# Gathering the token rows of two 64-expert mixtures on TensorE instead of through DRAM

## What is computed

```python
def hier_moe(h, w_rg, b_rg, w_re, b_re, w_gate, w_up, w_down, ws_gate, ws_up, ws_down, w_sg):
    xt = h.reshape(-1, D)                                   # 512 tokens x 1024
    g_sel = jnp.argmax(xt @ w_rg + b_rg, axis=-1)           # one of 8 groups
    ...                                                     # top 2 of the 8 experts of that group, softmax gates
    buf = jnp.zeros((P, D), xt.dtype).at[dest].set(xt[tok_sorted])     # rows of each expert together
    ...
    hid = jax.nn.silu(xb @ w_gate[e]) * (xb @ w_up[e])      # per expert: 1024 -> 256
    return hid @ w_down[e]                                  # 256 -> 1024
    ...
    y = jnp.zeros((N, D), xt.dtype).at[tok_sorted].add(out[dest] * gate_sorted[:, None])
    ys = (jax.nn.silu(xt @ ws_gate) * (xt @ ws_up)) @ ws_down          # shared expert, 1024 -> 512 -> 1024
    y = y + jax.nn.sigmoid(xt @ w_sg) * ys
```

## Time and profile before

| | |
|---|---|
| three runs | 2607.84, 2610.89, 2621.81 us (median 2610.89) |
| span of the profiled execution | 2608.0 us |
| share of the span: PE, DVE, ACT, POOL | 83%, 48%, 30%, 8% |
| DMA over the span | 684.69 MB, mean 263 GB/s |
| first 64-expert mixture | about 1036 to 1562 us |
| second 64-expert mixture | about 2039 to 2604 us |

### The profile page before, as it was taken

One profiled execution on the slowest core, in us unless ns is written; L12 is line 12 of the kernel. 1 busy time (PEld: TensorE's weight loads), 2 busy tenths in 40 slices (PEclk: granted clock), 3 DMA queues, 4 the chain that ended last, 5 costly groups with the idle time before them and its releaser, 6 DMA issues. The chain is left out here.

```text
span 2608.0 us, 43437 instructions
## 1 busy us (share of the span) xinstructions
PE 2153.1 (83%) x18242; PEld 1504.7 (58%) x18242; DVE 1246.3 (48%) x1974; ACT 776.7 (30%) x1304; POOL 210.0 (8%) x204
## 2 busy tenths in 40 slices
PE   5999999896884999887778766899998887768766
PEld 3977777794542789443334335677777644334433
DVE  3367676645223544543333336666545653233334
ACT  4266666432113323211111114444423411111112
POOL 2010000101001000000000002111111000000001
PEclk8999999998997999998889888999999999889988
DMA  9157675439997323899999973211113699999995
GB/s 356 46 195 245 219 245 188 130 98 365 420 421 266 97 97 126 352 411 416 419 419 417 415 320 98 58 46 46 50 50 130 258 386 416 415 414 420 409 417 205
DMA packets 211851, 684.69 MB, mean 263 GB/s; under 512 B 23022, under 2 KB 122039, under 8 KB 152503
## 3 DMA queue, kind: packets, MB, share of 16 engines
q1 hardware_dynamic: 198742, 646.01, 64.3%
q0 software_dynamic: 8912, 21.04, 2.2%
q10 hardware_dynamic: 3984, 14.68, 1.4%
HBM read 671.68 MB, written 21.00 MB: 266 GB/s over the span
## 5 line engine op out<-in xcount | busy, mean ns | idle before, releaser
L221 PE MATMUL PS<-second 128*128 128x256 f32 (+1 forms) x4944 | 929.8, 346 | 54.5 <-DVE second L251 21.7
L221 PEld LDWEIGHTS PS<-second 128*128 128x128 f32 x4944 | 760.1, 193 | 200.8 <-DVE second L251 29.1
L221 PE MATMUL PS<-ring,arena 128*32 128x256 f32 (+5 forms) x6288 | 670.2, 457 | 208.4 <-DMA ring<-in_moe_w_down 65.6
L221 PEld LDWEIGHTS PS<-ring,arena 128*32 128x32 f32 (+2 forms) x6288 | 317.1, 125 | 445.8 <-issue 306.2
L221 PE MATMUL PS<-arena 128*32 128x256 f32 (+10 forms) x2480 | 500.6, 386 | 76.7 <-DMA ring<-in_moe_w_up 20.3
L221 PEld LDWEIGHTS PS<-arena 128*32 128x32 f32 (+4 forms) x2480 | 248.4, 153 | 243.4 <-issue 173.5
L233 ACT ACTIVATE arena<-PS 128x256 f32<-128x256 f32 (+2 forms) x218 | 106.6, 489 | 575.3 <-PE PS L221 497.9
L240 DVE TENSOR_TENSOR arena<-PS,arena 128x512 f32<-128x512 f32 (+1 forms) x305 | 210.6, 690 | 98.5 <-PE PS L221 71.4
L240 DVE TENSOR_TENSOR arena<-arena,PS 128x256 f32<-128x256 f32 (+1 forms) x77 | 41.0, 532 | 403.6 <-PE PS L221 402.4
L233 ACT ACTIVATE arena<-arena 128x128 f32<-128x128 f32 (+4 forms) x299 | 176.3, 590 | 191.9 <-DVE arena L240 64.7
L240 DVE TENSOR_TENSOR second<-ring,second 128x1024 fp32r<-128x1024 f32 (+1 forms) x90 | 149.1, 1656 | 155.0 <-ACT second L233 149.1
(11 more groups left out here) (170 smaller groups left out, 1355.9 us busy)
## 6 DMA issues: line engine op xcount, KB each, us to landing
ring<-in_moe_w_down SPq DMA_DIRECT2D x124, 1024.0 KB, 14.3
ring<-in_moe_w_up SPq DMA_DIRECT2D x121, 1024.0 KB, 14.2
ring<-in_moe_w_gate SPq DMA_DIRECT2D x109, 1024.0 KB, 16.3
ring<-in_ada_w SPq DMA_DIRECT2D x48, 1024.0 KB
arena<-in_moe_w_gate SPq DMA_DIRECT2D x28, 1024.0 KB, 8.6
ring<-in_w_mod SPq DMA_DIRECT2D x22, 1024.0 KB, 9.8
arena<-in_moe_w_up SPq DMA_DIRECT2D x19, 1024.0 KB, 11.0
spare<-in_moe_w_gate SPq DMA_DIRECT2D x17, 1024.0 KB
```

What stands on the lines that cost most here:

```text
L221: return P.e.matmul(o, l, r, start=st, stop=sp)
```

## The change

The two 64-expert mixtures no longer store `XN` and no longer use indirect transfers. The 16-expert mixture keeps both. For each unit DVE builds a matrix `HOT` of 512 tokens by 128 rows (four blocks of 128 tokens): it compares the row numbers with each token's place, once for each of its two experts, multiplies by the token's 1/rms, and adds the two (`hot_ve`: nine instructions and one small one). `turn_pe` then makes the transposed rows directly, as products of the raw tokens `x` (stationary, every eighth feature of a row, so elements 32 bytes apart) with `HOT` (moving): 8 blocks of features by 4 blocks of tokens, 32 float32 products of 128 by 128 by 128 in place of eight transposes. DVE may start on its half after the first 16 of them.

In the head `turn_pe(0)` moves ahead of `tokens_pe` and of two steps of the shared expert. SP's wait for the store is gone. In `SIDE` the units 11 to 14 have 1, 1, 1, 1 steps in place of 2, 2, 0, 0. POOL's work in these mixtures is down to one row and the final products.

```diff
@@ new buffers
+    HOT = [view(16384 + 512 * i, 4, 128) for i in range(2)]
+    HOTB = spare[:, 2048:2560].rearrange("p (t r) -> p t r", t=4)
...
-    SIDE = (1, 2, 1, 2, 2, 1, 2, 1, 0, 2, 2, 2, 2)
+    SIDE = (1, 2, 1, 2, 2, 1, 2, 1, 0, 2, 2, 1, 1, 1, 1)
@@ begin_sp
-        S.wait_ge(at("xn_d", m.i), at("ps", "h2T", m.i, 3, 1))
+        S.wait_ge(at("ps", "h2T", m.i, 3, 1))
@@ turn_pe
+        if m.shared:
+            P.wait_ge(at("hot", m.i, n))
+            for k in range(8):
+                for t in range(4):
+                    i = mm((ba, bb)[k // 4][:, (k % 4) * 128:(k % 4) * 128 + 128], x[:, t, :].rearrange("q (p k) -> q k p", k=8)[:, k, :], HOT[n % 2][:, t, :], t == 0, t == 3)
+                if k % 4 == 3:
+                    i.then_inc(*P.mark("ps", "turn" if k == 7 else "turn0", m.i, n))
+            return
@@ moe_pe
         positions_pe(m)
         next(more, None)
+        if m.shared:
+            turn_pe(m, 0)
         tokens_pe(m, "tok", 0, m.NS)
...
@@ new: hot_ve, spots_ve
+    def hot_ve(m, n):
+
+        ts(m.near, m.spot, -128.0 * n, None, ALU.add, None)
+        V.wait_ge(at("ps", "turn", m.i, n - 2) if n > 1 else None, V.here())
+        for t in range(4):
+            for j, o in enumerate((HOT[n % 2], HOTB)):
+                V.e.tensor_scalar(o[:, t, :], iota[:, :], m.near[:, t, j:j + 1], rs[:, 4 + t:5 + t], ALU.is_equal, ALU.mult).then_inc(*V.mark())
+        tt(HOT[n % 2], HOT[n % 2], HOTB, ALU.add, "hot", m.i, n)
+
+    def spots_ve(m):
+        stt(m.spot, m.uu, 128.0, m.rr, ALU.mult, ALU.add)
@@ row_hots
         tt(m.rr, m.rr, m.ff, ALU.add)
+        if m.shared:
+            spots_ve(m)
+            if label[0] == "ohtok":
+                hot_ve(m, 0)
@@ moe_ve, in the loop over units, and in one(n) for the overflow units
+            if m.shared and n + 1 < m.NP:
+                hot_ve(m, n + 1)
             gate_up_ve(m, n)
...
         def one(n):
+            if m.shared:
+                hot_ve(m, n)
             turn_ve(m, n)
@@ h2T_ac
-        A.wait_ge(at("xn", m.before, t))
-        A.e.dma_start(xn_d[128 * t:128 * t + 128, :], XN[:, t, :]).then_inc(*D(f"xn_d{m.i}").next("xn_d", m.i))
+        if m.shared is None:
+            A.wait_ge(at("xn", m.before, t))
+            A.e.dma_start(xn_d[128 * t:128 * t + 128, :], XN[:, t, :]).then_inc(*D(f"xn_d{m.i}").next("xn_d", m.i))
```

More of the change, by code:

```diff
@@ L174, in program @@
     names_of_loads = ("xc", "xl", "stage", "rows", "z0", "z1", "zq", "x", "wba", "x2", "router0", "router1", "router2",
-                      "xn_d0", "xn_d1", "xn_d2", "y0", "y1", "xg0", "xg1", "xg2", "x_d", "out", "zero", "ab_d", "abp")
+                      "xn_d0", "y0", "y1", "xg0", "xg1", "xg2", "x_d", "out", "zero", "ab_d", "abp")
     d_sem = {n: sem("d_" + n) for n in names_of_loads}
     d_comb = [sem(f"d_comb{i}") for i in range(8)]
-    d_over = [[sem(f"d_over{j}_{i}") for i in range(n)] for j, n in enumerate((8, 8, 8))]
+    d_over = [[sem(f"d_over{i}") for i in range(8)]]
     def at(*label):
@@ L1448, in __init__ @@
                 self.tokf, self.ws = tmp(NB, 4), tmp(NB)
+                self.spot, self.near = tmp(4, 2), tmp(4, 2)
             self.tz, self.idx = tmp(NB), tmp(NB).bitcast(i32)
@@ L1824, in moe_pe @@
             row_pe(DIAG, ("row", m.i), state["side"])
-        turn_pe(m, 0)
+            turn_pe(m, 0)
         for n in range(m.NP):
@@ L1873, in turn_ve @@
         i, b = n % 2, bank("ta", m.i, n)
-        V.wait_ge(at("ps", "turn", m.i, n), at("ps", "gu", m.i, n - 2, 1) if n > 1 else None)
+        V.wait_ge(at("ps", "turn0" if m.shared else "turn", m.i, n), at("ps", "gu", m.i, n - 2, 1) if n > 1 else None)
         for k in range(4):
@@ L1982, in index_ve @@
         ts(m.tz[0:m.R, n0:n1], b, 0.0, 5000.0, ALU.is_equal, ALU.mult)
-        stt(m.idx[0:m.R, n0:n1], b, -1.0, m.tz[0:m.R, n0:n1], ALU.add, ALU.add, label, m.i)
         if m.shared:
             stt(m.tz[:, n0:n1], b, -1.0, m.tz[:, n0:n1], ALU.add, ALU.add, {"idx": "tokf", "idx2": "tokf2"}[label], m.i)
+        else:
+            stt(m.idx[0:m.R, n0:n1], b, -1.0, m.tz[0:m.R, n0:n1], ALU.add, ALU.add, label, m.i)
     def columns_ve(m, n0, n1):
@@ L2053, in route_ve @@
         ts(m.bb, m.pp, float(m.C), None, ALU.is_ge, None)
-        stt(m.rr, m.bb, 1000.0, m.pp, ALU.mult, ALU.add)
+        stt(m.rr, m.bb, 65536.0, m.pp, ALU.mult, ALU.add)
         row_hots(m, "ohtok", m.i)
-        index_ve(m, "tok", 0, m.NS, "idx")
+        if m.shared is None:
+            index_ve(m, "tok", 0, m.NS, "idx")
     def gates_of_ve(m, step):
@@ L2138, in moe_ve @@
         gates_of_ve(m, 0)
+        if m.shared:
+            turn_ve(m, 0)
+            index_ve(m, "tok", 0, m.NS, "idx")
         more_places_ve(m, 0)
         more = shared_ve(m) if m.shared else iter(())
-        turn_ve(m, 0)
+        if m.shared is None:
+            turn_ve(m, 0)
         gates_of_ve(m, 1)
@@ L2327, in moe_gp @@
         fill(m.M[:, 4:5], 0.0, "mz", m.i)
[L2328 to L2331, removed]
+        if m.shared:
+            G.wait_ge(at("sq2", m.before, 3), at("ps", "gu", m.i, 1, 1))
             row_gp(m.gate_col, DIAG, ("row", m.i))
[L2333 to L2343, removed]
             for t in range(4):
@@ L2347, in moe_gp @@
             return
+        for o in XG:
+            fill(o, 0.0, "zx", m.i)
+        G.wait_ge(at("sq2", m.before, 3))
+        row_gp(m.gate_col, DIAG, ("row", m.i))
+        for n in range(m.NP):
+            gather_gp(m, n)
+            if n == 6:
+                row_gp(colD[:, 64:72], DIAG, "frow", at("ps", ("row", m.i), 1))
+        count = count_of(m, G)
+        overflow(m, G, count, lambda n: gather_gp(m, n))
         G.wait_ge(at("yi", m.i), at("y", m.i, m.NB - 2), at("y", m.i, m.NB - 1))
@@ L2563, in gates_first_ve @@
     def gates_first_ve():
-        V.wait_ge(at("ps", "cm", 1, MO[1].NB - 1, 3, 1), at("passed", 1), V.here())
+        V.wait_ge(at("ps", "cm", 1, MO[1].NB - 1, 3, 1), V.here())
         V.e.memset(WBA[:, :, 16:32], 0.0).then_inc(*V.mark("wba0"))
```

## The result

The changed kernel takes 2843.8 us (median of 4 runs), the kernel before 2616.4 in the same session: a ratio of 1.088 (95% interval 1.0859 to 1.09), slower by some 228 us. The prediction was 2639 us, with a range of 2600 to 2700. The side was right; the size is that of rival B, and more than its outer end. The kernel before is timed anew in each session, and its median goes from 2611 to 2622 us between them, so sessions are best compared by their ratios.

A forecast was written before the change was run, and what follows sets the result against it. The weight stream was taken as the bound in the middle and end of mixtures, with PE slack there. First mixture +10.7, second +8.3 and overflow unit +8.7 us made 2639 us from 2610.9; range 2600 to 2700.

The forecast's parts named there:

- rival B: Turn's strided operand is slow: at 11.0 us a turn PE becomes the bound, 2673 us; chance 0.17.
- outer end: Strided operand at twice the price, 14.4 us a turn: 2787 us; chance 0.06, left out of the range.
- the term for the product: In each turn, 32 float32 products at 0.225 us take 7.2 us, 6.1 more per unit; no cost for the stride.
- My bound above, 1.5 times: Upper price of the strided read in the turn, from DVE's rows at this stride: 11.0 us a turn.
- Cover in the middle: Mid-mixture the turn costs nothing: a unit with two shared steps takes PE 29.8 us, the stream needs 30.2.
- 318 us: PE's work for all units of a mixture without turns, counted from the first gate product.
- The head: At each mixture's start, piece 3 of the shared weights is issued later: 8.8 us in the first, 9.0 in the second.
- Idle stream and gathers: Per mixture: stream idles for buffers in units 0 to 2, +11.2 and +8.6 us; removed gathers give -9.3 each.
- The overflow unit: At the end, one-hot, turn and combination delay gate 16 with no load covering it: +8.7 us.
- The sum: Whole kernel: 10.7 + 8.3 + 8.7 = +27.7 us on 2610.9, so 2639 us; chance 0.58.
- Rival C: Product is cheap, 0.13 us like a transpose, 4.2 us a turn: 2618 us, no change to tell; chance 0.12.
- D: Stream absorbs the head; PE's later turns don't reach it, only removed bytes count: 2592 us; chance 0.13.

The follow-up runs named there:

- contig: The changed kernel with the turn's stationary operand read as 128 features side by side, not every eighth (wrong features reach the experts): 2633.3 us, ratio 1.009 to before.
- stride2: The changed kernel with the turn's stationary operand read at every second element, 8 bytes apart (other features than the reference's): 2644.1 us, one time.
- stride4: The changed kernel with the turn's stationary operand read at every fourth element, 16 bytes apart (other features than the reference's): 2831.0 us, one time.
- no_gathers: The kernel before, without the indirect transfers of units 2 to 15 of both 64-expert mixtures (wrong expert inputs): 2591.5 us, ratio 0.9893.
- quarter: The contig kernel with only the first of four token blocks in each turn, 8 products in place of 32: 2594.9 us, one time.
- moving_contig: The changed kernel with the one-hot stationary and 512 side-by-side features moving, 8 products a turn (result not transposed, wrong data): 2630.8 us, one time.

## Why the prediction was right or wrong

- **The step that failed** is the term for the product: "Below, I take no cost", so 7.2 us a turn. It is 15.5. Of the two readings of DVE's rows that I wrote down, the one that I preferred (one element per cycle, so nothing to pay) doesn't carry over to PE. My bound above, 1.5 times, was taken from DVE too and was too low. The Trainium skill's rule stood on its page (Memory Cachelines) with no factor, and I gave it 0.17. Here contig, stride2 and stride4 show that two elements in 16 bytes or one is what decides, by a factor of 2.1.
- **Cover in the middle.** "In the middle of a mixture this costs nothing" hung on the 7.2. With 15.5 the 29.8 us of a unit become 38.1, and PE is the bound: rival B. Its arithmetic at 15.5 us a turn gives +97 us a mixture and +17 at the overflow unit, so some 2820. The measured +111.3, +103.7 and +17.6 show what it lacks: it prices work and no waits. The recorded terms of its 318 us add to 316. These plus 15 x 15.5 are 548.5 from the first gate product at 1091.0, so 1639.5, and the last weights are used at 1657.1. Between 1091 and 1657 PE waits 29.5 us in all, so the work itself was priced some 12 us too high. More than half of the waits, 16.3 us, are for DVE's copy of the hidden values; before, these were 3.6 us (from 1130 to 1560). The waits from 1130 to 1650 us:

```profile
PE PS L221 <- DVE arena L259: 16.3, 12, 2.3
PE PS L221 <- DMA ring<-in_moe_w_down: 5.7, 2, 4.5
```

- **The head.** In contig, where the turn has the price that I took, piece 3 comes 7.6 us later from the place product in the first mixture (forecast 8.8) and 11.8 in the second (forecast 9.0). Of this, 2.5 us are the clock, which the forecast had not: the same 98 records, from the turn on, took 15.11 us in the first at a granted clock of 1.00, and 17.63 in the second, where PE had waited 3.72 us before them and the clock was at 0.50 until 2074. Making `HOT` takes 3.1 us (forecast 2.9).
- **Idle stream and gathers.** From piece 3 to the last weights contig takes 0.7 us less than before in the first mixture (forecast +11.2 - 9.3 = +1.9) and 3.5 less in the second (forecast -0.7). With the 10.0 and 12.3 us that no_gathers saves there, the idle added is 9.3 and 8.8 us; the forecasts were 11.2 and 8.6.
- **The overflow unit** costs 11.2 us in contig, for 8.7: its turn took 9.36 us, not 7.2, since PE had waited 5.54 us and the clock was granted at 0.50 for the first 3.8 us of the turn. In the changed kernel it is 17.6.
- **The sum.** Forecast +28 us with a cheap turn: 2639. contig, which has it, took 2633, +21 us by both its median and its span. The terms measured above add to 26.4; the rest, -5.3, lies outside these stretches and has no cause that I can show. So the structure of the sum holds, and that the total came within 7 us is in part luck: -1.2 and +2.8 us in the two times of piece 3, -2.6 and -2.8 from there to the last weights, +2.5 at the overflow unit, and this -5.3.
- **A reading.** The earlier trace rows give 409 to 420 GB/s inside the two mixtures, not 410 to 422; nothing hangs on it.
- **Hidden work.** DVE's one-hots in the loop show no cost: the nine matrices that it makes between 1130 and 1500 us in the changed kernel are 32 us by their own durations, on an engine busy in 137 of 370, and PE waits for none of them there. Rival C falls (7.4 us a turn at best), and so does D: quarter shows all seven turns on the path.

## What to carry to other kernels

Before a product reads a float32 operand in place with a stride, ask how many of its elements share 16 bytes. With two the stationary operand cost 5% more, with one it cost twice, and at 32 bytes the moving operand cost twice too. A price seen on one engine is not that of another: 1.5 times on DVE, 2.1 on PE. Work moved to an engine with slack is free only as long as the unit stays under the stream's, so use it where the slack is: confined to the middle, the gather on PE made the kernel 0.8% faster; used in the heads and at the end too, where nothing covers it, 0.9% slower, even side by side. If a stretch is bound by loading, count its pieces as well as its bytes.

## What the runs showed of the hardware that I had not expected

- A float32 product of 128 by 128 by 128 takes 0.232 us with the stationary operand side by side, 0.244 at 8 bytes, 0.475 at 16 and 0.484 at 32.
- A moving operand of 512 elements pays the same: 0.446 us a record at 4 bytes, 0.933 at 32.
- The strided turn does not feel PE's clock. At the overflow unit PE has waited 5.54 us in both kernels and the clock starts at 0.50; the 64 records then take 9.36 us side by side (7.41 at full clock) and 15.51 at 32 bytes (15.50). The windows of the two turns, contig first; the third number from the end is the granted clock:
```profile
2579.20:2588.60 9.40, 9.40 (x65) 9.39 (x66) 1.64 (x4) 0.01 (x1) 0.00 (x0) 0.78 0.29 121
2786.80:2802.40 15.60, 15.54 (x65) 15.57 (x66) 1.64 (x4) 0.00 (x0) 0.00 (x0) 0.85 0.22 90
```
- Weights in pieces of 1 KB, with a third of the loads still in pieces of 8 KB, streamed at 367 GB/s, for 411 with 8 KB.
- Two executions can differ by some us in stretches with the same work: from the last weights of the first mixture to the place product of the second it was 516.2 us in the changed kernel, 515.6 in moving_contig and 509.0 in contig, which have the same instructions there. So differences of a few us are read inside a mixture here, not from spans.
